# Zero-padding the K=64 and K=48 products of a transformer-plus-SSM kernel to all 128 partitions, with narrower masks

## The reference, cut to what matters

```python
# attention, per head h and half n (64 features each), causal by chunks of 64 tokens
scores = einsum('bhnqd,bhnkd->bhnqk', qb, kb) * scale
mask = k_chunk[None, :] <= q_chunk[:, None]
probs = softmax(where(mask, scores, -inf)); attn = probs[:, :, 0] - lam * probs[:, :, 1]
...
# SSD, per head: only a difference of cumulative sums enters the decay matrix
seg = where(mask, a_cs[..., :, None] - a_cs[..., None, :], -inf); lmat = exp(seg)
...
# mLSTM, per head
dmat = where(mask, bcum[..., :, None] - bcum[..., None, :] + i_c[..., None, :], -inf)
w = exp(dmat - m_t[..., None]); s = einsum('blhd,bshd->bhls', q_c, k_c) * w
```

## Time and profile before

| | us |
|---|---|
| median of three runs | 1051.09 |
| lowest, highest run | 1049.94, 1052.87 |
| profiled execution, first to last instruction (span) | 1048.3 |
| TensorE matmul busy | 1025.7 (98%) |
| VectorE busy | 842.9 (80%) |
| ScalarE busy | 665.9 (64%) |
| GpSimd busy | 33.2 (3%) |

### The profile page before, as it was taken

How to read it: one execution, slowest core, us unless ns; L and a number is a source line. 1 busy time by engine, 2 the same in 40 slices (tenths; PEclk the granted TensorE clock), 3 DMA queues, 4 the chain that set the end, 5 groups by cost and what they waited for, 6 DMA issues and landing times. The chain is left out here.

```text
span 1048.3 us, 14957 instructions
## 1 busy us (share of the span) xinstructions
PE 1025.7 (98%) x5574; PEld 866.8 (83%) x5574; DVE 842.9 (80%) x1091; ACT 665.9 (64%) x834; POOL 33.2 (3%) x40
## 2 busy tenths in 40 slices
PE   7999999999999999999999999999999999999997
PEld 6778999999999888989879777777878777878784
DVE  5856776766777777787868799999999999999977
ACT  5554755555565755565544677777777777777764
POOL 1001000000000100100210000000000000000000
PEclk9999999999999999999999999999999999999999
DMA  9734456474624445333214889898989898989881
GB/s 346 264 121 141 140 182 224 143 236 146 217 86 161 161 162 166 121 122 122 81 33 167 323 318 376 353 383 348 385 349 386 349 385 346 381 353 386 346 328 44
DMA packets 82711, 253.62 MB, mean 242 GB/s; under 512 B 4160, under 2 KB 42176, under 8 KB 62656
## 3 DMA queue, kind: packets, MB, share of 16 engines
q1 hardware_dynamic: 82624, 252.50, 64.4%
HBM read 251.44 MB, written 1.05 MB: 241 GB/s over the span
## 5 line engine op out<-in xcount | busy, mean ns | idle before, releaser
L1064 DVE TENSOR_TENSOR WL<-raw,WH 128x2048 fp32r<-128x2048 f32 x230 | 493.7, 2176 | 92.1 <-ACT WH L544 92.0
L544 ACT ACTIVATE WH<-raw 128x2048 fp32r<-128x2048 f32 x231 | 419.6, 1823 | 126.3 <-PE bank L2000 80.5
L1998 PE MATMUL bank<-WH,MXH 128*128 128x512 f32 x552 | 226.3, 410 | 0.2 <-DVE WL L1064 0.2
L2000 PE MATMUL bank<-WH,MXL 128*128 128x512 f32 x552 | 215.2, 390 | 0.0
L1999 PE MATMUL bank<-WL,MXH 128*128 128x512 f32 x552 | 215.0, 390 | 0.0
L1998 PE MATMUL bank<-HTH,WH 128*128 128x256 f32 x576 | 165.3, 287 | 2.4 <-DVE HTL L1087 1.2
L1999 PE MATMUL bank<-HTL,WH 128*128 128x256 f32 x576 | 162.9, 283 | 0.0
L2000 PE MATMUL bank<-HTH,WL 128*128 128x256 f32 x576 | 162.9, 283 | 0.0
L1998 PE MATMUL bank<-WH,HTH 128*128 128x512 f32 x348 | 140.2, 403 | 1.4 <-DVE WL L1111 1.0
L1999 PE MATMUL bank<-WL,HTH 128*128 128x512 f32 x348 | 135.7, 390 | 0.0
L1998 PEld LDWEIGHTS bank<-WH,MXH 128*128 128x128 f32 x552 | 103.7, 188 | 27.2 <-issue 7.0
(11 more groups left out here) (396 smaller groups left out, 1105.0 us busy)
## 6 DMA issues: line engine op xcount, KB each, us to landing
raw<-in_exp_w_up SPq DMA_DIRECT2D x52, 1024.0 KB, 8.1
raw<-in_exp_w_gate SPq DMA_DIRECT2D x52, 1024.0 KB, 8.3
raw<-in_exp_w_down SPq DMA_DIRECT2D x52, 1024.0 KB, 6.8
raw<-in_w_in SPq DMA_DIRECT2D x34, 1024.0 KB, 5.3
raw<-in_w_up SPq DMA_DIRECT2D x22, 1024.0 KB, 5.3
raw<-in_w_down SPq DMA_DIRECT2D x11, 1024.0 KB, 5.1
raw<-in_w_out SPq DMA_DIRECT2D x8, 1024.0 KB, 5.0
raw<-in_w_o SPq DMA_DIRECT2D x4, 1024.0 KB, 5.7
```

Source lines behind the costliest of these rows:

```text
L544: e.activation(WH[i % HL][:, 0:n], raw[i % RAW][:, 0:n], ACT.Copy).then_inc(a_wh, 1)
L1064: e.tensor_tensor(l, r, h.bitcast(F32), ALU.subtract).then_inc(v_wl, 1)
L1998: e.matmul(out_, ah, bh, start=start, stop=False)
L2000: return e.matmul(out_, al, bh, start=False, stop=stop)
```

## The change

All products with fewer than 128 partitions in these three places take 128, the rest being zeros. For the scores the queries now lie in two tiles `QN`: half 0 in `RT8` with its lower 64 partitions cleared, half 1 in `Q2`, a part of the idle buffer `H`, with its upper 64 cleared; the keys are not touched. For the row products `rowsT` and `esel` get 128 partitions. The masks lose their empty part: the attention mask is 64 columns wide, written by a stride-0 pattern to two column groups (64 to 127 and 320 to 383); the mLSTM mask is 128 wide on two groups (0 to 127 and 256 to 383). Both masks now come last in their accumulation group. GpSimd clears three areas at the very start, and two waits on `g_zero` are new.

```diff
-        RND = sb("RND", 792, dt=F32R)
+        RND = sb("RND", 536, dt=F32R)
...
+        Q2 = H[:, 0, :].rearrange("p (h s) -> p h s", s=S)
+        QN = (RT8[:, 0:4, :], Q2)
...
-        rowsT, esel, ident_r, neg_r = RND[0:48, 0:256], RND[0:48, 256:280], RND[:, 280:408], RND[:, 408:792]
+        rowsT, esel, ident_r, neg_r = RND[:, 0:256], RND[:, 256:280], RND[:, 280:408], RND[:, 408:536]
...                                            # ScalarE
-            e.activation(mask[:, 128:512], const("chm", 384), ACT.Copy).then_inc(a_mask, 1)
+            e.activation(mask[:, 128:192], const("chm", 64, 64), ACT.Copy).then_inc(a_mask, 1)
...
-                    e.activation(RT8[:, 4 * c:4 * c + 4, t * 128:(t + 1) * 128],
-                                 bank[2 + t][:, :].rearrange("p (k s) -> p k s", k=4), ACT.Copy).then_inc(a_rtc, 1)
+                    src, ts = bank[2 + t][:, :].rearrange("p (k s) -> p k s", k=4), slice(t * 128, (t + 1) * 128)
+                    if c:
+                        e.activation(RT8[:, 4:8, ts], src, ACT.Copy).then_inc(a_rtc, 1)
+                    else:
+                        e.activation(QN[0][0:64, :, ts], src[0:64], ACT.Copy)
+                        e.activation(QN[1][64:128, :, ts], src[64:128], ACT.Copy).then_inc(a_rtc, 1)
...
-            e.activation(esel, cn[0:48, CN["esel"]:CN["esel"] + 24], ACT.Copy).then_inc(a_cum, 1)
+            e.activation(esel, const("esel", 24), ACT.Copy).then_inc(a_cum, 1)
...
-            e.activation(neg_r, const("neg", 384), ACT.Copy).then_inc(a_cum, 1)
+            e.activation(neg_r, const("neg", 128), ACT.Copy).then_inc(a_cum, 1)
             e.wait_ge(p_cum, P_CUM["turned"])
-            e.activation(rowsT, bank[1][0:48, 0:256], ACT.Copy).then_inc(a_cum, 1)
+            e.wait_ge(g_zero, 3)
+            e.activation(rowsT[0:48, :], bank[1][0:48, 0:256], ACT.Copy).then_inc(a_cum, 1)
...                                            # GpSimd, ahead of everything else
+            e.memset(QN[0][64:128, :, :], 0.0).then_inc(g_zero, 1)
+            e.wait_ge(g_zero, 1)
+            e.memset(QN[1][0:64, :, :], 0.0).then_inc(g_zero, 1)
+            e.wait_ge(g_zero, 2)
+            e.memset(rowsT.bitcast(F32), 0.0).then_inc(g_zero, 1)
+            e.wait_ge(g_zero, 3)
             e.wait_ge(d_cn, 16)
...                                            # TensorE, scores
-                    q, k = RT8[64 * n:64 * n + 64, h, :], RT8[64 * n:64 * n + 64, 4 + h, :]
-                    e.matmul(b[:, 0:384], mask[:, 0:128], mask[:, 128:512], start=True, stop=False)
-                    e.matmul(b[:, 0:128], q[:, 0:128], k[:, 0:128], start=False, stop=False)
-                    e.matmul(b[:, 128:384], q[:, 128:256], k[:, 0:256], start=False, stop=True).then_inc(p_score, 1)
+                    q, k = QN[n][:, h, :], RT8[:, 4 + h, :]
+                    e.matmul(b[:, 0:128], q[:, 0:128], k[:, 0:128], start=True, stop=False)
+                    e.matmul(b[:, 128:384], q[:, 128:256], k[:, 0:256], start=False, stop=False)
+                    late = b[:, :].rearrange("p (a b) -> p a b", a=2)[:, :, 64:128]
+                    e.matmul(late, mask[:, 0:128], bc(mask[:, 128:192].unsqueeze(1), P, 2, 64), start=False,
+                             stop=True).then_inc(p_score, 1)
...
             e.wait_ge(a_mask, 2)
+            e.wait_ge(g_zero, 2)
...                                            # TensorE, row products
-                return esel[:, k:k + 1].broadcast_to([48, 128])
+                return esel[:, k:k + 1].broadcast_to([P, 128])
...
-                e.matmul(b[:, 0:384], ident_r, neg_r, start=True, stop=False)
-                e.matmul(b[:, 0:128], row_of(16 + h), rowsT[:, 0:128], start=False, stop=False)
-                e.matmul(b[:, 128:384], row_of(16 + h), rowsT, start=False, stop=True).then_inc(p_mld, 1)
+                e.matmul(b[:, 0:128], row_of(16 + h), rowsT[:, 0:128], start=True, stop=False)
+                e.matmul(b[:, 128:384], row_of(16 + h), rowsT, start=False, stop=False)
+                own = b[:, :].rearrange("p (a b) -> p a b", a=2)[:, :, 0:128]
+                e.matmul(own, ident_r, bc(neg_r.unsqueeze(1), P, 2, 128), start=False, stop=True).then_inc(p_mld, 1)
```

More of the change, by code:

```diff
@@ L442, in build @@
             sem("v_" + n) for n in ("xtl", "route", "sel", "xst", "gm", "xc", "gs", "hid", "hil", "yg", "yl", "xg", "fo"))
-        g_rstd, g_xsd, g_vm, g_vc, g_wr, g_yz = (sem("g_" + n) for n in ("rstd", "xsd", "vm", "vc", "wr", "yz"))
+        g_rstd, g_xsd, g_vm, g_vc, g_wr, g_yz, g_zero = (sem("g_" + n) for n in ("rstd", "xsd", "vm", "vc", "wr", "yz",
+                                                                                "zero"))
         own_v, own_a = (sem("own_" + n) for n in "va")
```

## The result

| | before | after |
|---|---|---|
| median (lowest to highest), us | 1051.07 (1049.94 to 1052.87) | 1043.48 (1042.83 to 1044.39) |
| span of the profiled execution, us | 1048.3 | 1042.6 |
| granted clock, mean | 0.998 | 0.998 |

The ratio is 0.9931, 95% interval 0.992 to 0.9943: 7.3 us less, from 6.0 to 8.4. The forecast was 1044.6, 6.5 less. In the pages and traces of the changed kernel the lines have moved: the triple is L2012 to L2014, scores L2117 and L2118 with their mask L2120, turns L2134, SSD rows L2333, mLSTM rows L2359 and L2360 with mask L2362, `ml_s` L2374 and L2375, the mLSTM turn L2384; on VectorE the split is L1072, the taps L1364, the convolved product L1382, the sums L1509, SSD L1481, the gated output L1458; on ScalarE the split is L547, tanh L750.

A forecast was written before the change was run, and what follows sets the result against it. TensorE bounds the kernel, stalling where product heights change. Scores keep 3.6 us, SSD and mLSTM together 2.9 of 6.6; the 6.5 us sum takes 1051.1 to 1044.6 us, range 1040.0 to 1048.0.

The forecast's parts named there:

- The price of a change of height: On TensorE, each change of partition count between neighbouring products costs 0.19 us, which equal heights remove.
- Scores, 3.6: Attention scores on TensorE: two height changes and a narrower mask save 0.45 us a half, 3.6 us over eight halves.
- The cover: At the attention turns, VectorE's difference of head 1 is in time by 0.5 us, so all 3.6 is kept.
- SSD, 3.0 on TensorE: SSD row products: two height changes a pair go, 0.38 us, 3.0 us over eight pairs.
- mLSTM, 3.6 on TensorE: mLSTM: two height changes and a narrower mask save 0.45 us a head, 3.6 us over eight heads.
- The own sum of 10.2: TensorE's total saving before anything is taken back: scores 3.6, SSD 3.0 and mLSTM 3.6 us.
- What is taken back, 3.7 of 6.6: In SSD and mLSTM, VectorE and ScalarE hold TensorE, so only 2.9 of 6.6 us are kept.
- VectorE's pace: VectorE's rhythm stays: 7.38 us from SSD pair 5 to pair 6, and 8.55 a head in mLSTM.
- TensorE's wait at head 0: At mLSTM head 0, TensorE was to wait more than 1 us for VectorE's sums (L1501 in the kernel before).
- the loop: VectorE and ScalarE turn in their own loop in SSD pairs 4 to 6 and bound mLSTM up to head 4.
- Hidden edits: ScalarE's added copies, at most 1.2 us, and GpSimd's clears, 2.0 us, fall in idle time and cost nothing.
- The narrow masks: Score and mLSTM masks with fewer columns save 0.07 us a half and 0.06 a head on TensorE.

The follow-up runs named there:

- experiment 4: Kernel before with nine stretches of 12 fp32r products, at one height or with heights in turns, in place of 21 warm-up products; 1073.59 us in its one run.
- experiment 8: Changed kernel with scores not padded: lower and upper 64-row halves in turns, each in its own bank, masks also 64-row; 1043.27 us, ratio 0.9931.
- experiments 6 and 7: Kernel before (6) and changed kernel (7), both without two of three shifted mLSTM convolution taps on VectorE; 1133.97 and 1124.59 us.
- Experiments 3 and 5 to 7: 3: kernel before, only SSD and mLSTM row products padded, 1047.68 us; 5: changed kernel, ScalarE's split moved ahead of the first tanh, 1041.22 us.
- experiment 2: Kernel before with only the masks changed: narrow, on two column groups, last in their group, heights unpadded; 1050.38 us, ratio 1.0006.
- experiment 1: Changed kernel with the masks of before, 384 columns and first in their group, so only heights are padded; 1044.58 us, ratio 0.9943.

## Why the prediction was right

- *The price of a change of height.* 0.19 by three places of the trace before, and 0.19 in the stretch of experiment 4, where nothing else changes. Padding alone keeps 6.0 of 7.3 us, so the cause was named rightly.
- *Scores, 3.6.* The halves are 0.77 apart, as forecast; 1.81 a block, and 3.6 behind the second. All of it was kept: there is no wait at the turns. The cover was thin: VectorE's difference of head 1 ends at 54.62 and TensorE comes for it at 55.02, 0.4 later (forecast 0.5), and experiment 8, which comes 1.2 sooner, waits there.
- *SSD, 3.0 on TensorE.* A pair gives 0.36, from -3.8 to -6.3 over seven pairs, against 0.38; the pair shown adds 0.28, forecast 0.24.
- *mLSTM, 3.6 on TensorE.* A head's block went from 1.45 to 1.01, against 1.00. The own sum of 10.2 is nearly borne out by experiments 6 and 7, 9.4 to 9.8.
- *What is taken back, 3.7 of 6.6.* This is the step on which the forecast stood or fell, since without it the answer would have been 10.2. 3.0 are kept from the second score block to the last mLSTM head, forecast 2.9. VectorE's pace is nearly unchanged (7.33, forecast 7.38; 8.55 a head, forecast the same); the gated output is 5.8 sooner (430.55 to 424.74), forecast 3.6 + 2.3; TensorE's wait at head 0 is 1.21, forecast more than 1; at head 4 0.50, forecast short. At head 2 it is 1.73, forecast 1.43 and 0.45, 1.88. Experiments 3 and 5 to 7 show the mechanism: padding the row products gives 2.9 with the loop as it is, and SSD and mLSTM together keep 6.0 in place of 3.0 when the loop is light.
- *Hidden edits.* The two added copies and their neighbours take 0.59 each, half height or not. The four end 2.41 after the first begins, the two of before 1.08: 1.3 more and not 1.2, and no wait answers to them. The three clears take 0.95, 0.94 and 0.32, in all 2.2 and not 2.0, and end at 3.07, 15 us ahead of the first real work of GpSimd.
- *The size.* 7.3 us by the ratio against 6.5; the interval of 6.0 to 8.4 holds the forecast, and the traces give 6.5 up to the last mLSTM head. Whether the 0.8 is more than scatter stays open. The span of 1041.8 was forecast from an execution without the wait in the last unit, and 1042.6 was measured in one with it.
- *Only near the mark.* The narrow masks were summed at 0.07 and 0.06 each, some 1.0 of the 10.2, as if they were free of height; on their own they give nothing that the time shows (experiment 2), and beside padding 0.4 us by the matched products (6.5 against 6.1 behind the last mLSTM head; the ratios' intervals overlap). In the scores this is near the forecast's 0.56 (3.5 against 3.1 behind the second block); in mLSTM the loop keeps it from counting.

## What to carry to other kernels

Look for weight loads that start late in the middle of a dense stream: where the partition count of neighbouring products changes between sizes that the engine treats as different, padding with zeros costs nothing in columns and gives back some 0.2 us a change at 2.4 GHz. Before summing such gains over a stage, take the period of the engine that answers from the trace: what TensorE gains beyond that period turns into its own waits, and the next gain is then an edit of the other engine's order (here one moved line, 1.9 us by the ratios, 2.7 by the matched products). Two independent 64-row products in turns on the two halves of the rows are cheaper still for TensorE than padding, if their reader can follow; here the time did not fall by it.

## What the runs showed of the hardware that was not expected

- *Side by side.* Products on rows 0 to 63 and 64 to 127, in turns and into different banks, overlap: 0.11 a product at a clock at which a full-height one takes 0.21 (experiment 4), and in float32 a score block in 1.88 in place of 3.07 (experiment 8). The Trainium skill, "TensorEngine Tiling (Array Packing)", Key Properties, says that different tiles can load and multiply in parallel; both runs agree.
- *Heights that are not different.* 48 with 64, and 96 with 128, change at no cost; 32 with 64 and 64 with 128 cost 0.19 (experiment 4, whose expectation had it so). The prediction's "a load is fetched ahead only while the height stays the same" is thus too wide: it is the change between some heights that costs.
- *Loads of the same rows.* The Trainium skill, "TensorE: Matmul & The Clock Gate", Part 3, The mechanism, lets a load overlap, in its list of what does, only when its row group differs, though the same section also names a background weight buffer as a way past. Here 12 full-height products with 12 loads of the same rows go at 0.12 each, and the padded score products at 0.11 for 128 columns: the measurement decides against the list.
- *The clock.* The granted clock fell to 1.2 GHz behind products that alternate in height, though TensorE's matmul records fill the time: in the first score block of experiment 2, and in experiment 4 at 302.9 and again at 316.5. The second fall of experiment 2 has a wait of 1.34 just ahead of it. The same products at one height (after, experiment 1) kept 2.4 GHz; but so did the kernel before, which alternates too, in both of its profiles. What decides it was not tried.
- *ScalarE's copies.* 64 partitions by 512 columns take 0.59, 128 by 512 0.60: the time goes by the columns.
